# Sample RWKV in a hybrid decoder step: state changes as 32-row products of four samples, old-state products that alternate between the two heads

## The reference, cut to what matters

```python
def wkv_scan(r, decay, k, v, kk, a, s0):
    def step(S, inp):
        r_t, w_t, k_t, v_t, kk_t, a_t = inp
        sk = jnp.einsum('bhij,bhj->bhi', S, kk_t)
        S = S * w_t[:, :, None, :] - sk[..., None] * (kk_t * a_t)[:, :, None, :] + v_t[..., None] * k_t[:, :, None, :]
        return S, jnp.einsum('bhij,bhj->bhi', S, r_t)
```

## Time and profile before

| | us |
|---|---|
| median of three runs | 1922.98 |
| lowest and highest | 1920.84, 1925.62 |
| profiled execution | 1916.84 |
| its span in the profile | 1915.0 |

### The profile page before, as it was taken

One profiled execution on the slowest core, in us unless ns is written; L12 is line 12 of the kernel. 1 busy time (PEld: TensorE's weight loads), 2 busy tenths in 40 slices (PEclk: granted clock), 3 DMA queues, 4 the chain that ended last, 5 costly groups with the idle time before them and its releaser, 6 DMA issues.

```text
span 1915.0 us, 41445 instructions
## 1 busy us (share of the span) xinstructions
PE 1796.3 (94%) x17032; PEld 1703.2 (89%) x17032; DVE 777.8 (41%) x1115; ACT 623.4 (33%) x825; POOL 534.4 (28%) x206
## 2 busy tenths in 40 slices
PE   6999999996889998989969999999989999999998
PEld 6999999996779898978758989897889999999998
DVE  4332023314464546452367272727456333113320
ACT  4332122223423232422144343525343333123321
POOL 2434333431212121210002222212033344333342
PEclk9999999998999999999789999998799999999999
DMA  4343234331433133321034444445243334333433
GB/s 158 110 131 126 102 120 131 121 117 64 161 118 105 61 131 123 111 75 48 34 133 182 150 167 164 154 160 220 103 178 117 114 120 133 120 103 120 131 128 114
DMA packets 52164, 237.45 MB, mean 124 GB/s; under 512 B 6992, under 2 KB 7632, under 8 KB 50512
## 3 DMA queue, kind: packets, MB, share of 16 engines
q1 hardware_dynamic: 44176, 219.40, 33.3%
q10 hardware_dynamic: 7872, 16.37, 2.3%
HBM read 217.98 MB, written 71.76 MB: 151 GB/s over the span
## 4 chain that ended last, share of the span: by engine, by line
issue 81%; POOL 14%; PE 4%; POOLq 1%; ACT 0%; ACTq 0%
POOL w_lo L325 14%; PE ps L338 4%; POOLq L632 0%; POOLq L324 0%; POOLq L2183 0%; POOLq L635 0%; ACT w_hi L320 0%; POOLq L325 0%; POOLq L631 0%; ACTq L319 0%; POOLq L2360 0%
## 5 line engine op out<-in xcount | busy, mean ns | idle before, releaser
L325 POOL TENSOR_TENSOR w_lo<-w_raw,w_hi 128x1024 fp32r<-128x1024 f32 (+1 forms) x202 | 534.2, 2645 | 1358.9 <-ACT w_hi L320 1358.9
L338 PE MATMUL ps<-h_hi,w_hi 128*128 128x288 f32 x2464 | 553.6, 306 | 32.4 <-DVE h_lo L455 11.0
L338 PE MATMUL ps<-h_lo,w_hi 128*128 128x288 f32 x2464 | 529.5, 297 | 0.0
L338 PE MATMUL ps<-h_hi,w_lo 128*128 128x288 f32 x2464 | 529.4, 297 | 0.0
L338 PEld LDWEIGHTS ps<-h_hi,w_hi 128*128 128x128 f32 x2464 | 399.7, 190 | 57.3 <-issue 19.7
L338 PEld LDWEIGHTS ps<-h_lo,w_hi 128*128 128x128 f32 x2464 | 399.7, 190 | 0.0
L338 PEld LDWEIGHTS ps<-h_hi,w_lo 128*128 128x128 f32 x2464 | 399.4, 190 | 0.0
L320 ACT ACTIVATE w_hi<-w_raw 128x1024 fp32r<-128x1024 f32 (+1 forms) x204 | 226.2, 1109 | 431.2 <-PE ps L338 414.1
L338 PE MATMUL ps<-g_hi,w_hi 128*128 128x288 f32 x704 | 151.5, 297 | 0.3
L338 PE MATMUL ps<-g_hi,w_lo 128*128 128x288 f32 x704 | 151.1, 296 | 0.0
L338 PE MATMUL ps<-g_lo,w_hi 128*128 128x288 f32 x704 | 151.0, 296 | 0.0
(11 more groups left out here) (362 smaller groups left out, 1999.0 us busy)
## 6 DMA issues: line engine op xcount, KB each, us to landing
w_raw<-in_w SPq DMA_DIRECT2D x172, 512.0 KB, 3.5
w_raw<-in_w SPq DMA_DIRECT2D x32, 704.0 KB, 4.1
kv<-in_kc SPq DMA_DIRECT2D x32, 576.0 KB, 6.0
kv<-in_vc SPq DMA_DIRECT2D x32, 576.0 KB, 7.4
cache_out<-in_cache SPq DMA_DIRECT2D x28, 576.0 KB
gates<-gate_out ACTq DMA_DIRECT2D x16, 288.0 KB, 2.1
gate_in<-gates SPq DMA_DIRECT2D x8, 576.0 KB, 5.3
cache_out<-in_cache SPq DMA_DIRECT2D x8, 480.0 KB
```

Of the source, the lines that this page charges most:

```text
L325: nc.gpsimd.tensor_tensor(w_lo[par_][:, 0:words], w_raw[par_][:, 0:words], w_hi[par_][:, 0:words].bitcast(F32), ALU.subtract).then_inc(lo_ ...
L338: last = nc.tensor.matmul(ps[:, b + c, 0:HC], w[par_][:, wk], a[:, k, c * HC:(c + 1) * HC], start=(first and k == 0), stop=(end and k == n ...
```

## The change

The mask `seq` goes from 8 samples to 4 (repeated for tokens 0 to 31 and 32 to 63). The products of the old state are issued with the two heads alternating. In the second set, all products of lines 1294 and 1295 now come first. The state changes take only the 32 tokens (32 partitions) of four samples for each matmul, with 256 columns; the two halves go to two banks (6 and 7, or 4 and 5), and the order alternates between quarters of the array. A spread now holds both heads of a pair for four samples in each half of the partitions, so two VectorE operations serve a pair. Buffers alternate by pair, and TensorE waits for the output copies before pair 1 writes banks 4 and 5.

```diff
-    put("seq", (np.arange(64)[:, None] // DS == np.arange(8)[None, :]))
+    put("seq", (np.arange(64)[:, None] % 32 // DS == np.arange(4)[None, :]))
...
-            for ct, h in HEADS:
-                for b in range(DB):
-                    c = slice(64 * ct + 8 * b, 64 * ct + 8 * b + 8)
-                    last = nc.tensor.matmul(ps[rows_of(h), 6, c], SST[rows_of(h), ct, 64 * b:64 * b + 64], SXK[rows_of(h), c],
-                                            start=True, stop=True)
+            for ct, b, h in ((ct, b, h) for ct in range(CT) for b in range(DB) for h in range(2)):
+                c = slice(64 * ct + 8 * b, 64 * ct + 8 * b + 8)
+                last = nc.tensor.matmul(ps[rows_of(h), 6, c], SST[rows_of(h), ct, 64 * b:64 * b + 64], SXK[rows_of(h), c],
+                                        start=True, stop=True)
...
-                    for b in range(DB):
-                        c = slice(64 * ct + 8 * b, 64 * ct + 8 * b + 8)
-                        last = nc.tensor.matmul(ps[rows_of(h), 3, c], SST[rows_of(h), ct, 64 * b:64 * b + 64],
-                                                SV[rows_of(h), ct, 3, 8 * b:8 * b + 8], start=True, stop=True)
+            for ct, b, h in ((ct, b, h) for ct in range(CT) for b in range(DB) for h in range(2)):
+                c = slice(64 * ct + 8 * b, 64 * ct + 8 * b + 8)
+                last = nc.tensor.matmul(ps[rows_of(h), 3, c], SST[rows_of(h), ct, 64 * b:64 * b + 64],
+                                        SV[rows_of(h), ct, 3, 8 * b:8 * b + 8], start=True, stop=True)
             last.then_inc(sem("smat"), 1)
-            for ct, h in HEADS:
-                pe.wait_ge(sem("s_spread"), 2 * ct + h + 1)
-                if ct >= 2:
+            for ct in range(CT):
+                pe.wait_ge(sem("s_spread"), ct + 1)
+                if ct == 1:
+                    pe.wait_ge(sem("o_new"), 1)
+                    pe.wait_ge(sem("o_sample"), 1)
+                elif ct >= 2:
                     pe.wait_ge(sem("s_new"), ct - 1)
-                o = ps[rows_of(h), 5 + ct % 2, :]
-                nc.tensor.matmul(o, TOS[1][:, hc(ct, h)], SPREAD[h][0], start=True, stop=False)
-                nc.tensor.matmul(o, TOS[2][:, hc(ct, h)], SPREAD[h][1], start=False, stop=True).then_inc(sem("s_dstate"), 1)
-                if h:
-                    fill(2)
+                for turn in range(2):
+                    for a in range(2):
+                        for h in range(2):
+                            q = h ^ turn
+                            toks = slice(32 * q, 32 * q + 32)
+                            last = nc.tensor.matmul(ps[rows_of(h), (6, 4)[ct % 2] + q, 0:256], TOS[1 + a][toks, hc(ct, h)],
+                                                    SPREAD[ct % 2][a][toks, 256 * h:256 * h + 256],
+                                                    start=(a == 0), stop=(a == 1), skip_group_check=True)
+                last.then_inc(sem("s_dstate"), 1)
+                fill(2)
...
             for ct in range(CT):
-                for h in range(2):
-                    if ct:
-                        dve.wait_ge(sem("s_dstate"), 2 * ct + h - 1)
-                    for a, src in ((0, SUU), (1, TOS[3])):
-                        ins = V.tensor_tensor(by_head(SPREAD[h][a]), src[:, hc(ct, h)].unsqueeze(1).to_broadcast([64, 8, 64]),
-                                              seq, ALU.mult)
-                    ins.then_inc(sem("s_spread"), 1)
-                    dve.drain()
+                if ct >= 2:
+                    dve.wait_ge(sem("s_dstate"), ct - 1)
+                for a, src in ((0, SUU), (1, TOS[3])):
+                    both = src[:, 128 * ct:128 * ct + 128].rearrange("p (h n) -> p h n", h=2)
+                    ins = V.tensor_tensor(by_sample(SPREAD[ct % 2][a]), both.unsqueeze(2).to_broadcast([64, 2, 4, 64]), seq, ALU.mult)
+                ins.then_inc(sem("s_spread"), 1)
+                dve.drain()
                 if ct:
                     new_state(dve, own, ct - 1)
...
-            own(V.tensor_tensor(SST[:, ct, :], SST[:, ct, :], ps[:, 5 + ct % 2, :], ALU.add))
+            own(V.tensor_tensor(two_of(SST[:, ct, :]), two_of(SST[:, ct, :]), ps[:, (6, 4)[ct % 2]:(6, 4)[ct % 2] + 2, 0:256], ALU.add))
```

More of the change, by code:

```diff
@@ L69 @@
                   ("m16", 64), ("m32", 64), ("m64", 64), ("SU", 64), ("IU", 128), ("SU8", 64), ("IU8", 64),
-                  ("seq", 8), ("id2", 64), ("reset", NT)):
+                  ("seq", 4), ("id2", 64), ("reset", NT)):
     KCOL[_name] = (_n, _w)
@@ L1419, in rwsam_dve, with by_sample @@
             dve.drain()
-            seq = K("seq", 64).unsqueeze(2).to_broadcast([64, 8, 64])
+            seq = K("seq", 64).unsqueeze(1).unsqueeze(3).to_broadcast([64, 2, 4, 64])
+            def by_sample(a):
+                return a.rearrange("p (h b n) -> p h b n", h=2, b=4)
             for ct in range(CT):
-                for h in range(2):
-                    if ct:
-                        dve.wait_ge(sem("s_dstate"), 2 * ct + h - 1)
-                    for a, src in ((0, SUU), (1, TOS[3])):
-                        ins = V.tensor_tensor(by_head(SPREAD[h][a]), src[:, hc(ct, h)].unsqueeze(1).to_broadcast([64, 8, 64]),
-                                              seq, ALU.mult)
-                    ins.then_inc(sem("s_spread"), 1)
-                    dve.drain()
+                if ct >= 2:
[5 more added lines that the diff above has]
+                dve.drain()
                 if ct:
@@ L1435, in new_state, with two_of @@
             V = nc.vector
-            dve.wait_ge(sem("s_dstate"), 2 * ct + 2)
-            own(V.tensor_tensor(SST[:, ct, :], SST[:, ct, :], ps[:, 5 + ct % 2, :], ALU.add))
+            dve.wait_ge(sem("s_dstate"), ct + 1)
+            def two_of(a):
+                return a.rearrange("p (q n) -> p q n", q=2)
+            own(V.tensor_tensor(two_of(SST[:, ct, :]), two_of(SST[:, ct, :]), ps[:, (6, 4)[ct % 2]:(6, 4)[ct % 2] + 2, 0:256], ALU.add))
             s3 = SST[:, ct, :].rearrange("p (b n) -> p b n", b=DB)
```

## The result

The changed kernel takes 1902.1 us (median of five runs, 1898.36 to 1904.45) where the kernel before takes 1920.84 us (also five, 1916.99 to 1925.62). The ratio is 0.9897 with a 95% interval of 0.9877 to 0.9918, so it is faster by 1.0%, 18.7 us by the medians. The forecast was 14.6 us less and a time of 1908 us. The sign was right and so was most of the mechanism; the size was too small. The median of 1902.1 stands on the low end of the range, 1902, and 0.9897 of 1920.84 us is 1901.0 us, just under it. A second set of five runs of the changed kernel gave 0.9896 (0.9877 to 0.9915).

What follows compares the result with a forecast made beforehand. TensorE, busy for 94% of the span, was taken as the bound. Terms -5.0 - 1.0 - 5.2 + 0 - 3.4 = -14.6 us from 1922.98 gave 1908.4, rounded to 1908 us; 80% range 1902 to 1916.

Steps and rivals of the forecast that it cites:

- The pace of small products: TensorE's small products: 57 ns a record within one array quarter, 28.5 ns when quarters alternate, at full clock.
- Rival 2: Old-state products: row halves writing one PSUM bank run in turn, 7.3 us less gain, 1915.5 us; chance 0.06.
- First set, -5.0: Old-state products of line 1281: 128 records with alternating heads take 3.65 us instead of 8.68.
- Filler and transposes, -1.0: TensorE between the two old-state sets, 5.75 us: less low clock saves 1.0 us, bounds -2.0 and 0.
- Second set, -5.2: Lines 1294, 1295 and 1298: 64-column products first, then alternating small ones, 5.5 us instead of 10.7.
- Wait for the first spreads, 0: From the last small product to the first state product: the 2.41 us wait stays the same.
- State loop, -3.4: Lines 1306 and 1307: 256-column records, two heads together at 1.72 us a ct, 17.8 us instead of 21.2.
- rival 4: More than forecast: clock stays at 1.00 or four 32-row combinations overlap, 1901 to 1904 us; chance 0.10.
- VectorE hidden: State loop: VectorE's 4 x 2.75 = 11 us is hidden behind TensorE, its last update under the last filler.
- rival 1: Small products: the clock falls at the start of each set, leaving about -4, 1919 us; chance 0.08.
- Rival 3: Small products: each quarter change waits for the product before, about 1952 us, from about 120 ns a record; chance 0.03.

Runs made afterwards that it cites:

- fill_mid: Changed kernel with the filler behind the first old-state set split, one slice moved to after 64 of the set's 128 records; 1899.83 us, one run.
- Experiment 3: Kernel before with the changed old-state sets; loop keeps 64-row products and four spreads, but awaits both heads' spreads and alternates heads; 1911.28 us, one run.
- fill_gap: Changed kernel with the first pair's filler moved ahead of the state loop, into the wait for the first spreads; 1899.70 us, one run.
- experiment 6: Changed kernel with each spread of the loop written once more by VectorE, into a tile nobody reads; 1906.03 us, one run.
- experiment 5: Changed kernel with a pair's 16 records ordered quarter by quarter; 1903.24 us, one run.

## Why the prediction fell short

- *The pace of small products*: right. 29 ns a record at full clock in both sets, as worked out from lines 848, 894 and 1229, and 53 at a granted clock of 0.52 (`fill_mid`) where the sum took 54. Rival 2, turns for row halves that write one bank, is refuted: line 1297 writes one bank from both and keeps 29 ns. The Trainium skill, TensorEngine Tiling (Array Packing), section Restrictions and Gotchas, says that different row tiles cannot access one PSUM bank at the same time. The trace does not agree where the two write different partitions, as here.
- *First set, -5.0*: measured -4.1. The mechanism was right; 0.9 us is the clock that fell inside the set: its last 1.6 us ran at half clock. In the profile in which it did not fall there, the set took 3.89 us.
- *Filler and transposes, -1.0*: measured +0.4. This term was mis-sized. I took half of the low clock to be gone; it was as long as before, 0.58 on the mean against 0.63. The clock fell 3.0 us into the small products though they came twice as densely, and a slice of filler among them did not prevent it.
- *Second set, -5.2*: measured -5.3. Its clock was 1.00 all through.
- *Wait for the first spreads, 0*: measured 0.
- *State loop, -3.4*: measured -7.8. **This is the step that failed.** I wrote of the pair "I take 1.72, since line 1306 shows two heads together and no row shows four". Four 32-row quarters run together: 1.03 us a pair at full clock and 1.93 at half, which is 5.0 us for four pairs instead of the 9.4 in the sum (3.44, 2.4 and twice 1.8). These 4.4 us are the whole miss of the loop. Some 0.7 of them are clock and not quarters: the clock was back before the second pair, whose price of 2.4 assumed half of it slow (1.72 at full clock, two at a time). The fillers were right (3.11 at half clock, 1.7 to 1.8 at full). The bound below it, half of 1.72, stood in the text and was given to rival 4, whose chance of 0.10 was too small. Experiment 3 shows the price that I took (1.87 us with two heads) where the split is absent.
- *VectorE hidden*: right, but with 0.15 us to spare at the mean product, and in `fill_gap` VectorE is the bound. What two spreads a pair give for certain is the start of the loop: both heads start after two operations, where they wait 1.2 us longer in experiment 6 and 1.4 in experiment 3. Whether four spreads would stay hidden behind the faster pairs is open, as said there.
- *Rivals 1 and 3*: rival 1 was right in that the clock falls, but it fell late in the first set and not at all in the second, so it cost 0.9 us and not the rival's 3.2 of the first set. Rival 3 is refuted by 29 ns. Its threshold of 120 ns was mis-added: its own terms, (17.6 + 3.4 + 5.8) / 256, give 105.
- *The size and the range*: the forecast of 1908.4 lies 7.4 us above 1901.0. Of these, 2.1 are the base, 1922.98 us from three runs and 1920.84 from five. Another 2.2 are the stage: 4.4 in the loop and 0.1 in the second set, less 0.9 in the first set and 1.4 in the filler. It was luck that the last two hid half of the loop's miss. The last 3.0 are the difference between the ratio's 19.8 us and the stage's 16.8, which the interval does not tell from nothing. So the loop's term is the step that failed, but it does not take the time out of the range alone: put right, it gives 1904.0. The low end of 1902 was rival 4's middle on the early base.

What stays open: why the clock falls inside the first set in one execution and at its end in another, what made the clock fall at all, since neither denser products nor filler among them prevented it, and whether the ratio's 3 us beyond the stage are more than scatter. Filler in the middle was tried in one size only.

## What to carry to other kernels

Small float32 products that stay in one array quarter stood 57 ns a record apart here, and 29 ns when neighbours lay in different quarters; the order is free to change where the outputs are independent. A product with 64 rows of which each output needs only half of the tokens can be cut into 32-row halves: the padding with zeros shrinks, and here four quarters worked at once. The halves wrote different banks; one bank for both was not tried. When the trace shows two quarters at once and the change opens four, put the price of four into the sum's likely range, not only into a rival. And when one engine's part becomes short, look at the other's: VectorE was hidden here by 0.15 us.

## What the runs showed of the hardware

- The four 32-row quarters ran at once in each of the three orders tried. With a quarter's four records in a row, records of other quarters, up to eleven places later in the program, had started before the first quarter's third (experiment 5).
- A stretch of 8-column products with no gap in it began at a granted clock of 2.4 GHz and ended at 1.2, at 29 ns a record (the first set of the changed kernel) as at 44 (the kernel before). The second set of the changed kernel kept 2.4 GHz to its end. In the changed kernel 12 filler records, four transposes and a part of the next filler ran at half clock (911.10 on) before it was back.
- Identical kernels differed by 8 us in span, 1896.6 and 1904.5, with the edited stage of the changed kernel within 0.1 us of itself and that of the kernel before within 1.7. A stage read in the profile resolves more than the whole time does, but not tenths of a microsecond where the clock falls inside it.
